# Expert biases: one load spread over the partitions and added by VectorE, in place of four products on TensorE

## What is computed

```python
def swiglu_clamped(h):
    glu = jnp.minimum(h[..., ::2], SWIGLU_LIMIT)
    lin = jnp.clip(h[..., 1::2], -SWIGLU_LIMIT, SWIGLU_LIMIT)
    return glu * jax.nn.sigmoid(SWIGLU_ALPHA * glu) * (lin + 1.0)

def expert_block(args):                 # xb: 128 rows x 1024, w1[e]: 1024 x 2048, w2[e]: 1024 x 1024
    xb, e = args
    hid = xb @ w1[e] + b1[e]            # b1[e]: 2048 values, the same for every row
    return swiglu_clamped(hid) @ w2[e] + b2[e]
```

## Time and profile before

| | |
|---|---|
| median of 3 runs | 3970.72 us (3968.79 to 3972.16) |
| the profiled execution | 3970.23 us, of which span 3968.5 us |
| granted TensorE clock, mean of the span | 0.893 of full speed |
| busy: PE, DVE, ACT, POOL | 85%, 60%, 40%, 5% of the span |
| moved by DMA | 639.93 MB, mean 161 GB/s |
| hardware queue (SP), software queue (POOL) | 38.0% and 6.4% of 16 engines' span |
| chain that ended last | PE 39%, with L1994 17% and L2011 9% of the span |

### The profile page before, as it was taken

The page is one execution under the profiler, slowest core; times in us unless marked ns, Lnnn a source line. Parts: engine busy times, 40 slices in busy tenths (PEclk is TensorE's granted clock), DMA queues, the critical chain, the costliest instruction groups (busy, mean ns, idle before and its releaser), DMA issues. The chain is left out here.

```text
span 3968.5 us, 43967 instructions
## 1 busy us (share of the span) xinstructions
PE 3361.4 (85%) x15758; PEld 2740.5 (69%) x15758; DVE 2384.5 (60%) x2343; ACT 1576.8 (40%) x1609; POOL 188.9 (5%) x209
## 2 busy tenths in 40 slices
PE   6955995878999865677899869885899999999996
PEld 5844984656787653565688757565788888888884
DVE  3356335534443435453566453455899999999995
ACT  2131212322223222232222221242677777777773
POOL 0000000000000000000000000000111111111110
PEclk9956977888999887788899979786999999999997
DMA  4200001312233310131355323003999999999994
GB/s 152 90 1 0 1 1 53 112 32 74 90 95 93 101 53 0 53 112 32 129 181 177 99 92 90 27 22 128 356 387 385 383 382 391 385 384 383 382 388 154
DMA packets 118914, 639.93 MB, mean 161 GB/s; under 512 B 13432, under 2 KB 13432, under 8 KB 68784
## 3 DMA queue, kind: packets, MB, share of 16 engines
q1 hardware_dynamic: 99168, 562.62, 38.0%
q0 software_dynamic: 19664, 76.19, 6.4%
HBM read 614.11 MB, written 24.64 MB: 161 GB/s over the span
## 5 line engine op out<-in xcount | busy, mean ns | idle before, releaser
L301 PE MATMUL banks<-x_scratch,chunk_split 128*128 128x512 f32 x3648 | 856.8, 396 | 74.3 <-DVE x_scratch L278 61.6
L301 PEld LDWEIGHTS banks<-x_scratch,chunk_split 128*128 128x128 f32 x3648 | 694.5, 191 | 234.1 <-DVE chunk_split L270 73.2
L1994 PE MATMUL banks<-pair_split,rows 128*128 128x512 f32 x3072 | 702.6, 389 | 0.0
L1994 PEld LDWEIGHTS banks<-pair_split,rows 128*128 128x128 f32 x3072 | 577.5, 188 | 120.3
L265 ACT CAST chunk_split<-weight_ring 128x1024 fp32r<-128x1024 f32 x248 | 258.9, 1047 | 728.8 <-PE banks L301 582.4
L270 DVE TENSOR_TENSOR chunk_split<-weight_ring,chunk_split 128x1024 fp32r<-128x1024 f32 x248 | 302.9, 1224 | 161.5 <-ACT chunk_split L265 154.6
L2011 PE MATMUL banks<-pair_split,hidden_t 128*128 128x512 f32 x1536 | 362.5, 395 | 6.1 <-DVE hidden_t L2106 6.1
L2011 PEld LDWEIGHTS banks<-pair_split,hidden_t 128*128 128x128 f32 x1536 | 285.2, 189 | 70.8 <-DVE pair_split L1773 6.6
L1773 DVE TENSOR_TENSOR pair_split<-mixed,pair_split 128x2048 fp32r<-128x2048 f32 x128 | 292.9, 2289 | 31.3 <-ACT pair_split L1768 29.6
L1773 DVE TENSOR_TENSOR pair_split<-scratch,pair_split 128x2048 fp32r<-128x2048 f32 x128 | 290.3, 2288 | 35.4 <-ACT pair_split L1768 35.4
L1773 DVE TENSOR_TENSOR pair_split<-weight_ring,pair_split 128x2048 fp32r<-128x2048 f32 x128 | 290.2, 2288 | 34.3 <-ACT pair_split L1768 34.3
(11 more groups left out here) (539 smaller groups left out, 3795.1 us busy)
## 6 DMA issues: line engine op xcount, KB each, us to landing
weight_ring<-in_weights SPq DMA_DIRECT2D x296, 512.0 KB, 3.6
mixed<-in_w SPq DMA_DIRECT2D x128, 1024.0 KB, 9.2
weight_ring<-in_w SPq DMA_DIRECT2D x128, 1024.0 KB, 7.7
scratch<-in_w SPq DMA_DIRECT2D x128, 1024.0 KB, 8.9
mixed<-in_w_ada POOLq DMA_DIRECT2D x48, 512.0 KB, 3.8
token_sums<-tables POOLq DMA_DIRECT2D x1, 2560.0 KB, 21.3
residual<-in_x POOLq DMA_DIRECT2D x1, 2048.0 KB, 13.5
scratch<-in_mem POOLq DMA_DIRECT2D x2, 1024.0 KB, 5.3
```

Of the source, the lines that this page charges most:

```text
L301: mm = pe.matmul(banks[:, j, 0:tokens], chunk_split[:, a, at:at + P], split[b][:, k, 0:tokens], start=(k, a, b) == (0, 0, 0), stop=(k, a) ...
L1994: mm = pe.matmul(banks[:, n, :], rows[:, a, k, :], pair_split[k % SLOTS][:, b, n * T:(n + 1) * T], start=False, stop=(k, a) == (KB - 1, 1))
```

## The change

The bias no longer goes through PE. SP loads an expert's 2048 values 128 times over, once to each partition, 1 MB to `b1_spread`, behind the eight `w1` loads of the item; DVE adds them while it reads the first product out of PSUM, to `glu` and `lin`, and then clamps these in place. The split table, its two copies in HBM, the pick matrix, ACT's copy and the four products are gone; the first matmul of the first product now starts the sums.

```diff
@@ routing, expert_items @@
-        b1_pick = rounded_tensor("b1_pick", SCR_AT + 29 * T, 4, P)
...
+        b1_spread, b1_landed, b1_added = region(SCR_AT + 29 * T, 4 * T), sem("b1_landed"), sem("b1_added")
...
-        def b1_high(act):
-            need(act, "b1_whole")
-            act.copy(b1_parts[0], b1_whole).then_inc(b1_turn, 1)
-
-        def b1_rest(dve):
-            dve.wait_ge(b1_turn, 1)
-            dve.tensor_tensor(b1_parts[1], b1_whole, b1_parts[0], ALU.subtract).then_inc(b1_turn, 1)
...
         def store_tokens(pool):
-            pool.memset(b1_rows, 0.0).then_inc(b1_zeroed, 1)
-            pool.wait_ge(b1_turn, 2)
-            for part in range(2):
-                pool.dma_start(b1_dram[part].rearrange("e (n t) -> (e n) t", n=4), b1_parts[part].bitcast(F32))\
-                    .then_inc(b1_stored, 16)
...
                     pe.wait_ge(rows_lo, count)
-                    pe.wait_ge(b1_copied, count)
-                    for n in range(4):
-                        mm = pe.matmul(banks[:, n, :], b1_pick[:, n, :], b1_split, start=True, stop=False)
-                    mm.then_inc(b1_used, 1)
...
-                                               start=False, stop=(k, a) == (KB - 1, 1))
+                                               start=(k, a, b) == (0, 0, 0), stop=(k, a) == (KB - 1, 1))
...
                 with act.Fori(0, last) as i:
-                    b1_copy(i + 3)
...
                 def hidden(count, used):
                     dve.wait_ge(pair_used, used)
+                    dve.wait_ge(b1_landed, count * 16)
                     halves = banks[:, 0:4, :].rearrange("p b (f two) -> p b f two", two=2)
-                    dve.tensor_scalar(glu.rearrange("p (b f) -> p b f", b=4), halves[:, :, :, 0], 7.0, None, ALU.min)\
-                       .then_inc(glu_ready, 1)
-                    dve.tensor_scalar(lin.rearrange("p (b f) -> p b f", b=4), halves[:, :, :, 1], 7.0, -7.0, ALU.min, ALU.max)\
-                       .then_inc(lin_ready, 1)
+                    biases = b1_spread.rearrange("p (b f two) -> p b f two", b=4, two=2)
+                    dve.tensor_tensor(glu.rearrange("p (b f) -> p b f", b=4), halves[:, :, :, 0], biases[:, :, :, 0], ALU.add)
+                    dve.tensor_tensor(lin.rearrange("p (b f) -> p b f", b=4), halves[:, :, :, 1], biases[:, :, :, 1], ALU.add)\
+                       .then_inc(b1_added, 1)
+                    dve.wait_ge(b1_added, count)
+                    dve.tensor_scalar(glu, glu, 7.0, None, ALU.min).then_inc(glu_ready, 1)
+                    dve.tensor_scalar(lin, lin, 7.0, -7.0, ALU.min, ALU.max).then_inc(lin_ready, 1)
...
@@ expert_loads @@
             def bias(e, i):
-                if not (isinstance(i, int) and i == 0):
-                    sp.wait_ge(b1_copied, i)
-                for part in range(2):
-                    src = b1_dram[part][e:e + 1] if isinstance(e, int) else b1_dram[part][bass.ds(e, 1)]
-                    sp.dma_start(b1_rows[32 * part:32 * part + 4, :], src.rearrange("a (n t) -> (a n) t", n=4))\
-                        .then_inc(b1_landed, 16)
+                if not isinstance(i, int):
+                    sp.wait_ge(b1_added, i)
+                src = d["b1"][e:e + 1] if isinstance(e, int) else d["b1"][bass.ds(e, 1)]
+                sp.dma_start(b1_spread, src.to_broadcast([P, 4 * T])).then_inc(b1_landed, 16)
...
             first(0, None)
-            sp.wait_ge(b1_stored, 32)
-            sp.wait_ge(b1_zeroed, 1)
             bias(0, 0)
             sp.wait_ge(items_ready, 1)
-            bias(expert(1), 1)
             last = last_item(sp)
             with sp.Fori(0, last) as i:
-                bias(expert(i + 2), i + 2)
                 first(expert(i + 1), i)
+                bias(expert(i + 1), i + 1)
                 second(expert(i), i, PAIRS_IN)
```

More of the change, by code:

```diff
@@ L1744, in program @@
         sums_landed, sums_turned, b2_ready, b2_added = sem("sums_landed"), sem("sums_turned"), sem("b2_ready"), sem("b2_added")
-        picked_ready, y_free = sem("picked_ready"), sem("y_free")
+        y_free = sem("y_free")
         h2_rows = nc.dram_tensor("h2_rows", (T + P, D), F32, kind="Internal").ap()
         sums = nc.dram_tensor("token_sums", (T + P, D), F32, kind="Internal").ap()
-        b1_dram = [nc.dram_tensor(f"b1_rows_{part}", (E_N, 4 * T), F32, kind="Internal").ap() for part in ("hi", "lo")]
         def pair_number(i, p):
@@ L1881, in dve @@
                 dve.tensor_scalar(dummy_row, vec("part"), float(T), None, ALU.add)
-                for n in range(4):
-                    L(dve.tensor_scalar(hot_work[:, 0:4, :].rearrange("p a b -> p (a b)"), vec("part").to_broadcast([P, P]),
-                                        float(n), None, ALU.is_equal))
-                    dve.scalar_tensor_tensor(b1_pick[:, n, :], vec("part").to_broadcast([P, P]), float(32 + n),
-                                             hot_work[:, 0:4, :].rearrange("p a b -> p (a b)"), ALU.is_equal, ALU.add)\
-                       .then_inc(picked_ready, 1)
-                    dve.wait_ge(picked_ready, n + 1)
                 dve.wait_ge(pe_step.sem, p0 + 1)
@@ L2047, in hidden_out @@
                     act.copy(hid_t[:, 0], banks[:, 6:8, :].rearrange("p b (k s) -> p (b k) s", s=P)).then_inc(hidden_hi, 1)
-                def b1_copy(count):
-                    act.wait_ge(b1_landed, count * 32)
-                    act.wait_ge(b1_used, count + (-1))
-                    act.copy(b1_split, b1_rows).then_inc(b1_copied, 1)
                 def y_out(i, used):
@@ L2060, in act @@
                 act.sem_inc(y_ready, 1)
-                act.wait_ge(b1_landed, 32)
-                act.copy(b1_split, b1_rows).then_inc(b1_copied, 1)
                 rows_to_split(1)
@@ L2479, in _pack @@
     out["b_router"] = a["b_router_2"].reshape(1, E_N)
-    out["w1"], out["b1"] = a["w1_2"][0].reshape(E_N * KB, P, 2 * D), a["b1_2"][0].reshape(E_N * 4, T)
+    out["w1"], out["b1"] = a["w1_2"][0].reshape(E_N * KB, P, 2 * D), a["b1_2"][0].reshape(E_N, 4 * T)
     out["w2"] = a["w2_2"][0].reshape(E_N * KB // 2, 2, P, D).transpose(0, 2, 1, 3).reshape(E_N * KB // 2, P, 2 * D)
```

5 lines of the change are left out of this document (removed).

## The result

The changed kernel takes 4033.26 us (median of 4 runs, 4030.15 to 4035.69), the kernel before 3969.8 us on the same chip: ratio 1.0159 (95% interval 1.0141 to 1.0176). It is slower by 63 us, against a forecast of 49 more. The profiled run took 4032.0 us, its span is 4030.3.

The account below looks back on a forecast made before the run. PE was taken to lead with the DMA engines level, DMA taking over after the change at 37.3 us per item. 30 x 1.85 + 1.9 - 7.6 = +49.8 us on 3970.72 gave 4020 us, range 3985 to 4070.

Parts of the forecast that it names:

- rival 3: Expert loop: PE's clock falls after a stall in each item, 1.7 us of products, period 38.1, 4045 us; chance 0.10.
- Bias products: PE in the expert loop: four products per item go, taking 0.92 us off the chain.
- The DVE chain: Adds and clamps on DVE: silu 1.93 us later, pair 11 late, PE stall 1.9 us per item, PE period 36.4 us.
- DMA's floor: Loop's DMA engines: 35.45 less 0.64 of dips plus 2.46 for the load, 37.3 us per item; by rate 34.4.
- Rival 1: Expert loop: PE chain alone paces at 36.4 us since DMA has room, 3993 us; chance 0.20.
- SP's new wait: SP waits for the previous item's adds before the bias load, second weights behind it; claimed to cost nothing.
- Rival 2: Bias load: the repeated row is read at half rate, 4.9 us of engine time, 4094 us; chance 0.13.
- Rival 4: Expert loop: adds hide under the second product and DMA has room, so the change wins, 3935 us; chance 0.06.
- First item: Start of the loop: earlier loads of item 1 gain 5.0 us, two bias products fewer 2.6, together -7.6 us.
- Tail: After the loop: the last item's longer DVE chain shows once more, +1.9 us.
- What would show it: Signs in the changed profile: 32 loads, full DMA share without dips, PE stall, ACT waiting for DMA, silu time, shorter first pause.
- 30 x 1.85: Loop term: thirty item periods, each 1.85 us longer at the DMA-set 37.3 us.

Follow-up runs that it names:

- neither: Changed kernel with bias loads for item 0 alone and clamps straight from PSUM, no bias added: 3934.45 us, ratio 0.9909 to the kernel before.
- no_adds: Changed kernel with the 1 MB bias load kept but the adds left out, clamps straight from PSUM: 3976.13 us, ratio 1.0016 to the kernel before.
- early_pair: Changed kernel, adds and load kept, with pair 11's high part and rest moved ahead of silu: 3980.42 us, ratio 1.0029 to the kernel before.
- one_load: Changed kernel with biases loaded for item 0 alone, both adds kept in every item: 3997.35 us, ratio 1.0067 to the kernel before.
- other_rows: Changed kernel whose 1 MB load reads 128 different first-weight rows instead of one row 128 times: 4032.01 us, ratio 1.0157 to the kernel before.
- glu_first: Changed kernel with DVE's order add glu, clamp glu, add lin, clamp lin: 4013.64 us, ratio 1.0110 to the kernel before.

## Why the prediction came out as it did

The forecast was 4020 us in a range of 3985 to 4070; measured were 4033.26. The sign and the size hold, and the terms beside the period were near. The step that set the period, DMA at 37.3 us, was wrong, and what stood in its place was in part rival 3. That the sum came out near is luck in this part.

- **Bias products, 0.92 us.** Right: the period of neither is 34.56 against 35.45, 0.89 less.
- **The DVE chain.** Right nearly to the hundredth. The add took 1.22 us, as priced by the row subtraction; the clamp from SBUF 0.69 (taken 0.75, ends 0.48 and 1.22); silu started 3.10 us after the first add (forecast 3.18); the stall with nothing else in play was 1.68 (forecast 1.9), and the PE chain's period 36.45 (forecast 36.4). The cover had been read rightly too: that pair 11 was already just in time.
- **DMA's floor.** Here the step failed. I took 37.3, because the share read 1.00 and only two dips of 0.64 us in all seemed free. With a queue kept full the same bytes go in 35.97 us (no_adds and early_pair), so that the room before the change was, with my 2.46 for the load, 35.45 + 2.46 - 35.97 = 1.94 us, three times what the dips told and half of what the rate told. A share of 1.00 to 1.02 was had at 385, 390 and 408 GB/s: it says that packets are under way, not that the engines can move no more. Rival 1 had this right, and would have given 3993; one_load, which has that chain and no load, took 3997.35.
- **What made up the difference.** With a chain of 36.45 over a floor of 35.97 the time should have been near rival 1's. It was not: in every second item pair 10 comes late from DMA, the adds start late behind it, and pair 11 and PE's stall with them. The likely reason, shown at its two ends alone, is that the longer DVE stretch also holds the raw buffers (SP's pair of loads spans 9.45 us, 7.59 without the adds), so that DMA runs short of work. I had written that SP's new wait costs nothing, and looked no further at who waits for buffers; that is the missing term.
- **Rival 3, the clock.** Right in kind: a late pair brings a stall of 1.94 to 2.94 us, and 3.4 us at half clock follow; they cost 1.4 to 1.6 us each (I took 1.7). Wrong in how often: in each second item, not in all 30, 24.5 us in sum. The deciding point was not the stall that I priced, which never lowered the clock in one_load, but the lateness on top. The Trainium skill (TensorE: Matmul & The Clock Gate, HAM oscillation) describes a loop in which the wait for each load sends the clock down anew, in every tile; the trace here agrees in kind, and differs in that only the longer of two alternating waits does so.
- **Rival 2.** Excluded by other_rows. **Rival 4, faster.** Excluded by the stall in every item; neither at 3934.45 is where it would have been (forecast 3935).
- **First item, -7.6 us.** Measured -8.1 at the start of the loop's first product, of which the first period gives 1.9 back, because that product now starts before the clock has risen; I had no term for this. PE's pause is 7.43 us instead of 12.20, and the hidden transposes start 8.46 us after the row transposes (forecast 8.3):

```profile
2783.56 1.04 PE L1953 MATMUL banks<-tables,normed 128*128 128x128 f32 x8
...
2792.02 1.94 PE L1970 MATMUL banks<-tables,scratch 128*128 128x128 f32 x8 [7.43 <-DVE rows L2050]
2793.61 23.95 PE L1964 MATMUL banks<-pair_split,rows 128*128 128x512 f32 x96
```

- **Tail, +1.9.** Measured +1.3.
- **What would show it.** Seen: the 32 loads, PE's stall by DVE, ACT waiting for DMA, silu's time, the first pause. Not seen: a DMA share without dips. The dips stayed, and that was the sign that DMA was not the bound that I had taken it for. And the granted clock fell below 1.00, which I had named as the sign for rival 3.

In the sum, 30 x 1.85 became 30 x 2.28. Thirty us of that are the PE chain, as worked out; where I had put 27 more for DMA (30 x 0.9) stood 24.5 of clock, 12 of late pairs and 2 of the first period. The forecast was near for a reason that was half wrong.

## What to carry to other kernels

Two costs that each look harmless can meet where one engine both does the new work and frees the buffers of the loads: ask how long no buffer comes free, and whether the queue lasts that long. Read DMA's room from a run with the same transfers in which its queue is never empty, since a busy share of 1.00 does not tell it. Before giving up a step for its length, look for an idle engine ahead of the one wait that it delays: here one step moved gave back 53 of 63 us. And a small transfer costs its time to landing where an engine's next instruction waits for it; issued 25 us early it costs nothing.

## What was not expected of the hardware

- A stall of 1.68 us per 36.45 us never lowered the granted clock, each of the 15 stalls of 1.94 to 2.94 us in the changed kernel did; yet in glu_first 12 of the 21 stalls of 1.73 to 2.63 us did not. The falls in the changed kernel's loop start 75.1 us from one another (once 78.5), more evenly than the stalls before them, which start 74.7 to 76.9 us apart. So the time at which a stall comes may decide beside its length; how is open.
- The DMA engines' mean share read 1.00 to 1.02 at 385, 390, 391 and 408 GB/s in four kernels with the same kinds of weight loads.
- One row read 128 times is as fast as 128 rows (4032.01 against 4033.26 us).
- Loads of 8 KB, behind loads of weights, took 4.4 to 6.0 us from issue to landing in three items looked at; issued just before ACT wanted them, they made the kernel 36 us slower.
